# The value products of a pair of attention steps, issued at the end of the same pair instead of a pair later

## The chip, the cores and the metric

The kernel runs on one core of a Trainium2 chip. The metric is the device time of one execution in microseconds (us). Before the change three runs took 1965.31, 1966.28 and 1966.82 us; their median, 1966.28 us, is the time before. Five engines work side by side, each through its own list of instructions, in order: TensorE (PE, matmuls and transposes), ScalarE (ACT), VectorE (DVE), GpSimd (POOL) and SyncE (SP, which here issues nearly all DMAs). They wait for each other by semaphores.

## The reference, cut to what matters

Two layers of a decoder, each with forgetting attention and a gated MLP beside it. The change lies in the attention over the 1024 prompt positions:

```python
def fox_prompt(q, k, v, logf):                 # q, k, v: (1, 1024, 8 heads, 64)
    c = jnp.cumsum(logf, axis=1).transpose(0, 2, 1)
    def block(i):                              # 128 queries
        s = jnp.einsum('bqhd,bkhd->bhqk', qb, k) * HEAD_DIM ** -0.5
        s = s + (cb[..., :, None] - c[..., None, :])
        s = jnp.where(qpos[:, None] >= kpos[None, :], s, -jnp.inf)
        p = jax.nn.softmax(s, axis=-1)
        return jnp.einsum('bhqk,bkhd->bqhd', p, v)
```

The same stage also computes the input projections of q, k, v of the later pairs of heads, and the two gates `sigmoid(g_a)` and `sigmoid(g_b)` (as tanh) of the merge, which are 2 x 1024 columns of the input projection. These are independent of the attention and fill TensorE between its steps.

## The kernel before, in words

Every product in float32 is made of three matmuls (`three`, L76 to L78): each operand is split in a high part that TensorE takes at full rate and a low remainder. ScalarE makes the high part (a copy), VectorE or GpSimd the low one (a subtraction).

`attention_plan` writes the order of the attention stage as a list of small tasks. Each engine walks that same list and does its own share of each task, so the list sets the order on every engine at once. The tasks:

- `S h i`: scores of head h, 128 queries i, against the keys up to them: one or two chunks of at most 512 columns (PE L1324, L1326, mask L1329). VectorE adds the decay and takes the maximum (L1221, L1228), ScalarE the exponential (L1035), VectorE the division by the sum (L1121, L1122). The chunks use two PSUM banks in turn, so a third chunk waits until VectorE has taken the first.
- `T h G j`: transposes of the probabilities, keys j against the 512 queries of half G (PE L1341, 1 to 4 transposes). ScalarE copies the high part out of PSUM (L1045, tile `pthi`), VectorE the low one (L1237, tile `ptlo`). Two PSUM banks, three slots in SBUF.
- `V h G j`: the value products of that step (PE L1354 with the high part, L1355 with the low part), summed over j in one PSUM bank. The copy L1045 of a step waits until the V three steps earlier is done, for its slot.
- `O h G`: after the last V of a half, ScalarE copies one half of the sum (L1054, tile `ao`), VectorE adds the other (L1244), SP stores it.
- `Z p t`: q, k, v projections of 128 rows for a pair of heads (24 matmuls L76 to L78 on `aw_whi`), then copies and norms on ScalarE, VectorE, GpSimd; `X p t`: transposes of the normed q and k (PE L1301) with their splits (ACT L1015, DVE L1176, L1178).
- `P b c half`: a half-chunk of the gates, 12 matmuls L76 to L78 on `fhi`, `flo`. Two halves fill one PSUM bank, and ScalarE empties it by a tanh, `E` (L989, tile `th`). Z and P share two banks in turn: the first half of a chunk, or a Z, waits until the user two before it has been emptied.
- `G`, `W`, `Y`: loads and splits of weights; `D`: store of a tanh tile.

There are 96 steps (8 heads, 4 + 8 per head), taken two at a time: 48 pairs. In this text pair n is the one with steps 2n and 2n+1, from pair 0 to pair 47, in each of the two layers. Before the change a pair is: the `X` that is due, the two `T`, the `E` of what is unread, the two `V` **of the pair before** (and its `O`), then the scores and projections that are due, mixed with half-chunks, and half-chunks until the share of filling work is used. `LAG = 2` is the distance in steps between T and V. On PE that is

    X  T T  V V (of the pair before)  S .. Z .. P P P

## Time and profile before

| | |
|---|---|
| median of three runs | 1966.28 us |
| the profiled execution | 1964.39 us, of which span of the trace 1962.7 us |
| PE busy | 1904.7 us (97%) |
| DVE, ACT, POOL busy | 962.8, 677.1, 519.7 us |
| granted TensorE clock, mean | 0.993 |

The profile is of one execution. In a row of the timeline the first number is the start in us from the span's start, the second the duration; brackets name what ended an idle time before it. The ends of matmuls are modelled, and they overlap: from start to start a matmul of 384 columns takes 0.17 us though its row says 0.34. So distances on PE are taken here from start to start. The attention loop of the first layer runs from 114 us to 516 us, that of the second from 1080 us to 1481 us.

### The profile page before, as it was taken

The page shows a single profiled execution, that of the slowest core. Times are in us where ns is not written, and L with a number is a line of the kernel's source. Part 1 is how long each engine was busy: PE and PEld are TensorE (multiplying, and loading weights), DVE is VectorE, ACT ScalarE, POOL GpSimd, SP SyncE. Part 2 cuts the span into 40 slices and gives each one's busy share as a digit, 9 for nine tenths or more (in the row PEclk, how much of TensorE's full clock was granted, in tenths as well). Part 3 has the DMA queues.
Part 4 walks back from the last instruction along what each step waited for, and adds up shares of the span by engine and source line. Part 5 has one row for each costly group of instructions (what it writes and reads, how often), then busy time and mean ns, then how long its engine had stood idle before and what let it go on. Part 6 is the DMA issues. An engine that isn't in the chain of part 4 may idle for free.

```text
span 1962.7 us, 30986 instructions
## 1 busy us (share of the span) xinstructions
PE 1904.7 (97%) x11188; PEld 1755.5 (89%) x11188; DVE 962.8 (49%) x2296; ACT 677.1 (34%) x1487; POOL 519.7 (26%) x525
## 2 busy tenths in 40 slices
PE   5999999999999999999999999999999999999998
PEld 4999999999888889998789999999997888999986
DVE  5555665653264335455444565666433633455531
ACT  5344444444233222113224444454433332221120
POOL 3623333332021113111135233333311211231110
PEclk9999999999999999999999999999999999999999
DMA  5231313133215323525214213131322352226141
GB/s 155 58 108 52 94 54 96 47 88 84 64 39 158 91 62 87 196 84 167 97 55 111 59 48 99 44 106 49 106 58 62 79 147 77 76 83 232 39 172 54
DMA packets 217803, 178.39 MB, mean 91 GB/s; under 512 B 50260, under 2 KB 191076, under 8 KB 217652
## 3 DMA queue, kind: packets, MB, share of 16 engines
q1 hardware_dynamic: 217652, 176.41, 30.8%
q8 instruction: 90, 1.47, 0.3%
q14 instruction: 61, 0.50, 0.1%
HBM read 131.65 MB, written 44.71 MB: 90 GB/s over the span
## 4 chain that ended last, share of the span: by engine, by line
PE 85%; DMA 4%; DVE 3%; issue 2%; ACT 2%; SPq 1%; POOL 1%; POOLq 0%; DVEq 0%; ACTq 0%
PE bank L76 23%; PE bank L77 22%; PE bank L78 22%; PE bank L1341 3%; PE bank L1355 2%; PE bank L1301 2%; PE bank L1354 2%; PE bank L1324 2%; PE bank L1326 2%; PE bank L2108 2%; PE bank L2131 1%; DMA me_stage<-in_w_proj_b 1%; PE bank L2096 1%; DMA wo_stage<-in_w_out 1%; DVE at_prob L1221 1%
## 5 line engine op out<-in xcount | busy, mean ns | idle before, releaser
L76 PE MATMUL bank<-keep_hhi,at_fhi 128*128 128x384 f32 (+1 forms) x768 | 257.0, 335 | 3.4 <-ACT at_th L989 3.1
L78 PE MATMUL bank<-keep_hhi,at_flo 128*128 128x384 f32 (+1 forms) x768 | 251.3, 327 | 0.0
L77 PE MATMUL bank<-keep_hlo,at_fhi 128*128 128x384 f32 (+1 forms) x768 | 251.3, 327 | 0.0
L76 PE MATMUL bank<-aw_whi,keep_hhi 128*128 128x384 f32 (+3 forms) x576 | 198.5, 345 | 3.2 <-ACT at_th L989 1.3
L76 PE MATMUL bank<-keep_hhi,bw_whi 128*128 128x384 f32 (+1 forms) x576 | 196.3, 341 | 0.5 <-DVE br_th L1996 0.5
L77 PE MATMUL bank<-aw_wlo,keep_hhi 128*128 128x384 f32 (+3 forms) x576 | 195.5, 339 | 0.0
L78 PE MATMUL bank<-aw_whi,keep_hlo 128*128 128x384 f32 (+3 forms) x576 | 195.4, 339 | 0.0
L77 PE MATMUL bank<-keep_hlo,bw_whi 128*128 128x384 f32 (+1 forms) x576 | 189.4, 329 | 0.0
L78 PE MATMUL bank<-keep_hhi,bw_wlo 128*128 128x384 f32 (+1 forms) x576 | 189.2, 328 | 0.0
L1035 ACT ACTIVATE at_prob<-at_prob,at_nmx 128x128 f32<-128x128 f32 (+7 forms) x128 | 99.5, 778 | 239.0 <-DVE at_nmx L1228 238.9
L76 PEld LDWEIGHTS bank<-keep_hhi,at_fhi 128*128 128x128 f32 x768 | 144.4, 188 | 6.6 <-ACT at_th L989 5.3
L1237 DVE TENSOR_TENSOR at_ptlo<-bank,at_pthi 128x512 fp32r<-128x512 f32 x192 | 99.5, 550 | 98.6 <-ACT at_pthi L1045 97.3
L77 PEld LDWEIGHTS bank<-keep_hlo,at_fhi 128*128 128x128 f32 x768 | 144.7, 188 | 0.2
L78 PEld LDWEIGHTS bank<-keep_hhi,at_flo 128*128 128x128 f32 x768 | 144.3, 188 | 0.0
L1081 POOL TENSOR_TENSOR at_flo<-at_stage,at_fhi 128x512 fp32r<-128x512 f32 x64 | 85.8, 1340 | 170.2 <-ACT at_fhi L971 169.8
L1045 ACT ACTIVATE at_pthi<-bank 128x512 fp32r<-128x512 f32 x192 | 90.8, 491 | 73.7 <-PE bank L1341 62.4
L76 PE MATMUL bank<-ow_w,keep_hhi 128*128 128x512 f32 (+1 forms) x288 | 113.9, 395 | 0.7 <-issue 0.7
L78 PE MATMUL bank<-ow_w,keep_hlo 128*128 128x512 f32 (+1 forms) x288 | 114.2, 397 | 0.0
L77 PE MATMUL bank<-ow_w,keep_hhi 128*128 128x512 f32 (+1 forms) x288 | 113.8, 395 | 0.0
L76 PEld LDWEIGHTS bank<-keep_hhi,bw_whi 128*128 128x128 f32 x576 | 109.3, 190 | 4.0 <-issue 1.0
L76 PEld LDWEIGHTS bank<-aw_whi,keep_hhi 128*128 128x128 f32 (+1 forms) x576 | 105.5, 183 | 7.0 <-ACT at_th L989 1.8
L77 PEld LDWEIGHTS bank<-keep_hlo,bw_whi 128*128 128x128 f32 x576 | 109.3, 190 | 0.0
(252 smaller groups left out, 4300.7 us busy)
## 6 DMA issues: line engine op xcount, KB each, us to landing
at_stage<-in_w_in SPq DMA_DIRECT2D x160, 128.0 KB, 2.3
mg_gate<-gates SPq DMA_DIRECT2D x32, 544.0 KB, 5.2
gates<-at_th SPq DMA_DIRECT2D x64, 192.0 KB, 2.3
br_stage<-in_w_in SPq DMA_DIRECT2D x40, 256.0 KB, 3.2
at_stage<-in_w_in SPq DMA_DIRECT2D x48, 192.0 KB, 2.6
at_decay<-ncum SPq DMA_DIRECT2D x16, 512.0 KB, 3.8
br_k<-in_cache_k SPq DMA_DIRECT2D x32, 256.0 KB, 3.0
br_v<-in_cache_v SPq DMA_DIRECT2D x32, 256.0 KB, 3.0
```

What stands on the lines that cost most here:

```text
L76: nc.tensor.matmul(out, sh, mh, start=start and i == 0, stop=False)
L77: nc.tensor.matmul(out, sh, ml, start=False, stop=False)
L78: last = nc.tensor.matmul(out, sl, mh, start=False, stop=stop and i == n - 1)
L1035: nc.scalar.activation(prob[:, blk(i):blk(i) + w], prob[:, blk(i):blk(i) + w], ACT.Exp, bias=nmx[:, si % 2:si % 2 + 1], accum_out=sm[:, si ...
L1045: nc.scalar.activation(pt_hi[:, ti % (LAG + 1), lo:512], tps[ti % 2][:, lo:512], ACT.Copy).then_inc(t_hi, 1)
L1081: nc.gpsimd.tensor_tensor(flo[:, fu % NF, :], stage[:, slot[s], :], fhi[:, fu % NF, :].bitcast(F32), ALU.subtract).then_inc(w_lo_p, 1)
L1237: nc.vector.tensor_tensor(pt_lo[:, ti % (LAG + 1), lo:512], tps[ti % 2][:, lo:512], pt_hi[:, ti % (LAG + 1), lo:512].bitcast(F32), ALU.sub ...
L1301: last = nc.tensor.transpose(xps[:, at:at + n], qn[0:n, 2 * i + hh, :, :].rearrange("p e d -> p (e d)"), g.ident[0:n, 0:n])
L1324: nc.tensor.matmul(sps[cc % 2][:, 0:w], qk[:, h % NHEAD, 0, q], qk[:, h % NHEAD, 1, ks], start=True, stop=False)
L1326: last = nc.tensor.matmul(sps[cc % 2][:, 0:w], qk[:, h % NHEAD, 0, q], k_lo[:, h % NHEAD, ks], start=False, stop=not diagonal)
L1341: last = nc.tensor.transpose(tps[ti % 2][:, r * P:(r + 1) * P], prob[:, at:at + P], g.ident[:, :])
L1354: nc.tensor.matmul(ops[:, lo:512], pair, pt_hi[:, ti % (LAG + 1), lo:512], start=j == 0, stop=False)
```

## The change

The loop over the pairs ends one pass earlier, and the `V` of a pair (with its `O`) is put behind that pair's own scores, projections and half-chunks. Only these lines of `attention_plan` differ; the number of instructions stays the same on every engine.

```diff
-    for n in range(0, len(steps) + LAG, 2):
+    for n in range(0, len(steps), 2):
         due = after.pop(n, []) + after.pop(n + 1, [])
...
         plan += [("T",) + s for s in steps[n:n + 2]]
         fill.read(0)
-        for h, G, j in steps[max(0, n - LAG):n - LAG + 2]:
-            plan.append(("V", h, G, j))
-            if j == 4 * G + 3:
-                plan.append(("O", h, G))
         while scores or projections:
...
         while spent + fill.at - first < total * (n + 2) / (len(steps) + 1) and fill.at < len(fill.pieces):
             fill.half()
+        for h, G, j in steps[n:n + 2]:
+            plan.append(("V", h, G, j))
+            if j == 4 * G + 3:
+                plan.append(("O", h, G))
```

A pair on PE is now `X  T T  S .. Z .. P P P  V V (of this pair)`. Since the V of a pair and the T of the next one have nothing between them but an X, the order of PE as a whole changes only in this: at each start of a pair, the X and the two T change places with the two V.

TensorE at the start of pair 12 (head 2, first half, keys 0 and 1), `-` before and `+` after. L77 and L78 are the end of the filling work of pair 11, L1341 the T of pair 12, L1354 and L1355 the V of pair 11, L1324 the scores of pair 12:

```order
 L77 MATMUL bank<-keep_hlo,at_fhi 128x320
 L78 MATMUL bank<-keep_hhi,at_flo 128x320
-L1341 MATMUL bank<-keep_ident,at_prob 128x128 x7
 L1354 MATMUL bank<-at_pthi,at_vsplit 128x256
 L1355 MATMUL bank<-at_ptlo,at_vsplit 128x256
 L1354 MATMUL bank<-at_pthi,at_vsplit 128x128
 L1355 MATMUL bank<-at_ptlo,at_vsplit 128x128
+L1341 MATMUL bank<-keep_ident,at_prob 128x128 x7
 L1324 MATMUL bank<-at_qk 128x512
 L1326 MATMUL bank<-at_klo,at_qk 128x512
```

The seven transposes move behind the four value matmuls, right in front of the scores; the scores and everything up to the next start of a pair stay where they were.

ScalarE at the same place. L1045 are the copies of the two T of pair 12, L989 the tanh of the two chunks that pair 11 left unread, L1054 the output copy of head 1; before the change:

```order
L1045 ACTIVATE at_pthi<-bank 128x512
L1045 ACTIVATE at_pthi<-bank 128x384
L989 ACTIVATE at_th<-bank 128x384 x2
L1054 ACTIVATE at_ao<-bank 64x512
```

The same stretch of ScalarE's list after the change:

```order
L1054 ACTIVATE at_ao<-bank 64x512
L1045 ACTIVATE at_pthi<-bank 128x512
L1045 ACTIVATE at_pthi<-bank 128x384
L989 ACTIVATE at_th<-bank 128x384 x2
```

The output copy moves ahead of the two copies of P and the tanh; nothing else moves on ScalarE here. On VectorE the sum L1244 likewise moves ahead of the X and T of the next pair:

```order
-L1176 TENSOR_TENSOR at_qk<-bank,at_qk 64x2x128
-L1178 TENSOR_TENSOR at_klo<-bank,at_qk 128x2x128
-L1237 TENSOR_TENSOR at_ptlo<-bank,at_pthi 128x512
-L1237 TENSOR_TENSOR at_ptlo<-bank,at_pthi 128x384
-L1244 TENSOR_TENSOR at_ao<-bank,at_ao 64x512
+L1244 TENSOR_TENSOR at_ao<-bank,at_ao 64x512
+L1176 TENSOR_TENSOR at_qk<-bank,at_qk 64x2x128
+L1178 TENSOR_TENSOR at_klo<-bank,at_qk 128x2x128
+L1237 TENSOR_TENSOR at_ptlo<-bank,at_pthi 128x512
+L1237 TENSOR_TENSOR at_ptlo<-bank,at_pthi 128x384
```

Here one instruction moves past four; the scores behind them keep their place. SP's stores of `ao` move in the same way; GpSimd's list does not change.

Of the kernel before, what the change touches and what calls it, by code (L numbers as in the profile page):

```python
# [562 lines left out]
LAG = 2  # L563
# [65 lines left out]
def attention_plan():  # L629

    plan = []
    fill = Filler(plan)
    for t in range(NT):
        plan.append(("Z", 0, t))
        if t >= 2:  # L640
            plan.append(("X", 0, t - 2))
        if t >= 3:
            fill.weights(min(t - 2, NF))
    plan += [("F",)]
    fill.half()
    plan += [("X", 0, NT - 2)]
    fill.half()
    fill.half()
    fill.read(0)
    plan += [("W", 1, k) for k in range(2)]  # L650
    fill.half()
    plan += [("X", 0, NT - 1), ("C",), ("N", 0)]
    for i in range(1, 4):
        fill.half()
        fill.read(0)
        plan += [("W", 1, k) for k in (2 * i, 2 * i + 1)]
        fill.half()
    fill.read(0)
    plan += [("S", 0, 0), ("S", 0, 1)]
    fill.half()  # L660
    plan += [("S", 0, 2)]
    fill.half()
    fill.read(0)
    plan += [("S", 0, 3)]
    fill.half()
    fill.half()
    after = {}
    PER = 12

    def put(n, *steps):  # L670
        after.setdefault(n, []).extend(steps)

    for h in range(H):
        for i, off in enumerate((-10, -9, -8, -6, -4, -3, -2, 0)):
            if h or i >= 4:
                put(max(0, PER * h + off), ("S", h, i))
    for p in range(1, PAIRS):
        at = [3, 5, 7, 9, 11, 13, 15, 17, 19]
        for t, n in zip(range(NT - len(at), NT), at):
            n += 2 * PER * (p - 1)  # L680
            put(n, ("Z", p, t))
            if t and ("X", p, t - 1) not in plan:
                put(n, ("X", p, t - 1))
        put(n + 2, ("X", p, NT - 1))
        if p + 1 < PAIRS:
            for k in range(KT):
                put(n + 1 + 2 * (k // 3), ("W", p + 1, k))
        else:
            for u in range(KT):
                put(n + 2 + 2 * u, ("Y", u))  # L690
    steps = [(h, G, j) for h in range(H) for G in range(2) for j in range(4 * G + 4)]
    first = fill.at
    total = sum(2 * (s[0] == "Z") for v in after.values() for s in v) + len(fill.pieces) - first
    spent = 0
    turned = []
    for n in range(0, len(steps) + LAG, 2):
        due = after.pop(n, []) + after.pop(n + 1, [])
        plan += turned
        turned = [s for s in due if s[0] == "X"]
        scores = [s for s in due if s[0] == "S"]  # L700
        projections = [s for s in due if s[0] == "Z"]
        plan += [("T",) + s for s in steps[n:n + 2]]
        fill.read(0)
        for h, G, j in steps[max(0, n - LAG):n - LAG + 2]:
            plan.append(("V", h, G, j))
            if j == 4 * G + 3:
                plan.append(("O", h, G))
        while scores or projections:
            if scores:
                s = scores.pop(0)  # L710
                plan.append(s)
                if s[2] == PT_ - 1 and s[1] + 1 < H:
                    plan.append(("N", s[1] + 1))
            if projections:
                fill.before_z()
                spent += 2
                plan.append(projections.pop(0))
            elif scores:
                fill.half()
        plan += [s for s in due if s[0] in "WY"]  # L720
        while spent + fill.at - first < total * (n + 2) / (len(steps) + 1) and fill.at < len(fill.pieces):
            fill.half()
    fill.end()
    assert not after
    return plan


def attention_phase(nc, l, g):
    plan = attention_plan()
    R = Region(nc, "at", g.free_attention)  # L730
    S = g.sem("a", l)
# [1742 lines left out]
```

How the kernel before makes its waits and increments, by code:

```python
def all_through(eng, g):  # L119
    eng.wait_ge(g.pe_through, g.phases)
    eng.wait_ge(g.act_through, g.phases)
    eng.wait_ge(g.dve_through, g.phases)
    eng.wait_ge(g.pool_through, g.phases)
    eng.wait_ge(g.sp_through, g.phases)
# [54 lines left out]
    @block.sync  # L181
    def _(sp):
        sp.dma_start(g.gains[0:DEPTH, :], norm_g[:, :]).then_inc(gains_in, 16)
        sp.dma_start(g.gains[DEPTH:DEPTH + 1, :], norm_g[0:1, :]).then_inc(gains_in, 16)
        for t in range(NT):
            if t >= NX:
                sp.wait_ge(hn_r, t - NX + 1)
                sp.wait_ge(ss_r, t - NX + 1)
            sp.dma_start(xt[0:ROWS[t], t % NX, :], x_rows(g, t)).then_inc(x_in[t % NX], 16)
            if t == 0:
                sp.wait_ge(gains_in, 32)
                sp.dma_start(gain[:, :], g.gains[0:1, :].to_broadcast([P, D])).then_inc(consts, 16)
            if t >= 3:
                load_pair(sp, g, 0, 0, t - 3, stage[:, t - 3, :], w_in[t - 3])
        for k in range(NT - 3, KT):
            load_pair(sp, g, 0, 0, k, stage[:, k, :], w_in[k])
        sp.sem_inc(g.sp_through, 1)
# [3 lines left out]
        def square(t):  # L201
            if t >= NT:
                return
            act.wait_ge(x_in[t % NX], 16 * (t // NX + 1))
            if t:
                act.wait_ge(ss_r, t)
            if t >= NR:
                act.wait_ge(ms_r, t - NR + 1)
            nc.scalar.activation(sqj[0:ROWS[t], :], xt[0:ROWS[t], t % NX, :], ACT.Square,
# [84 lines left out]
    @block.tensor  # L294
    def _(pe):
        pe.wait_ge(made, 3)
        for t in range(NT):
```

## Rows read from the trace of the kernel before

**Rows 1.** Waits of PE, whole span: who, for whom; us, times, longest.
```profile
PE bank L76 <- ACT at_th L989: 4.4, 8, 1.0
...
PE bank L1324 <- DVE at_mx L1221: 3.7, 6, 1.0
```

**Rows 2.** ScalarE's copy L1045: what ended the idle time before it, us, times.
```profile
  PE bank L1355: 8.9, 34
```

**Rows 3.** Timeline of PE, start of pair 12: transposes, then the gate half-chunk.
```profile
220.11 0.93 PE L1341 MATMUL bank<-keep_ident,at_prob 128*128 128x128 f32 x7
...
222.33 0.41 PE L76 MATMUL bank<-keep_hhi,at_fhi 128*128 128x384 f32 x1
```

**Rows 4.** Timeline of ScalarE, start of pair 12: copies of P, tanh.
```profile
220.75 1.12 ACT L1045 ACTIVATE at_pthi<-bank 128x512 fp32r<-128x512 f32 x2 [0.50 <-PE bank L1341]
221.76 0.82 ACT L989 ACTIVATE at_th<-bank 128x384 f32<-128x384 f32 x2
```

**Rows 5.** Timeline of PE, end of pair 47: last value products, last half-chunk.
```profile
513.40 0.28 PE L1354 MATMUL bank<-at_pthi,at_vsplit 128*128 128x256 f32 x1
...
513.81 0.36 PE L76 MATMUL bank<-keep_hhi,at_fhi 128*128 128x320 f32 x1
```

**Rows 6.** Timeline of ScalarE, same place: the output copy behind them.
```profile
514.01 0.59 ACT L1054 ACTIVATE at_ao<-bank 64x512 f32<-64x512 f32 x1 [1.68 <-PE bank L1355]
```

**Rows 7.** Timeline of PE, start of pair 37: T, V, S, P.
```profile
428.96 0.49 PE L1341 MATMUL bank<-keep_ident,at_prob 128*128 128x128 f32 x3
429.20 0.48 PE L1354 MATMUL bank<-at_pthi,at_vsplit 128*128 128x512 f32 x1
...
430.11 0.22 PE L1324 MATMUL bank<-at_qk 128*128 128x128 f32 x1
...
430.73 0.41 PE L76 MATMUL bank<-keep_hhi,at_fhi 128*128 128x320 f32 x1 [0.17 <-ACT at_th L989]
```

**Rows 8.** Timeline of ScalarE, start of pair 37.
```profile
429.37 0.38 ACT L1045 ACTIVATE at_pthi<-bank 128x256 fp32r<-128x256 f32 x1 [1.47 <-PE bank L1341]
430.02 0.28 ACT L1045 ACTIVATE at_pthi<-bank 128x128 fp32r<-128x128 f32 x1 [0.26 <-PE bank L1355]
430.19 0.87 ACT L989 ACTIVATE at_th<-bank 128x384 f32<-128x384 f32 x2
```

**Rows 9.** Timeline of PE, start of pair 39.
```profile
444.83 1.03 PE L1341 MATMUL bank<-keep_ident,at_prob 128*128 128x128 f32 x8
...
447.45 0.41 PE L76 MATMUL bank<-keep_hhi,at_fhi 128*128 128x320 f32 x1
```

**Rows 10.** Timeline of PE, start of pair 44.
```profile
483.62 1.04 PE L1341 MATMUL bank<-keep_ident,at_prob 128*128 128x128 f32 x8
...
486.02 0.45 PE L76 MATMUL bank<-keep_hhi,at_fhi 128*128 128x384 f32 x1 [0.96 <-ACT at_th L989]
```

**Rows 11.** Timeline of PE, start of pair 47.
```profile
505.66 0.49 PE L1341 MATMUL bank<-keep_ident,at_prob 128*128 128x128 f32 x3
...
507.37 0.44 PE L76 MATMUL bank<-keep_hhi,at_fhi 128*128 128x384 f32 x1 [0.41 <-ACT at_th L989]
```

**Rows 12.** Timeline of ScalarE, start of pair 39: the tanh.
```profile
446.92 0.87 ACT L989 ACTIVATE at_th<-bank 128x384 f32<-128x384 f32 x2
```

**Rows 13.** Timeline of VectorE, pair 26: its two low parts of P.
```profile
340.78 1.27 DVE L1237 TENSOR_TENSOR at_ptlo<-bank,at_pthi 128x512 fp32r<-128x512 f32 x2
```

**Rows 14.** Timeline of PE: the start of pair 27.
```profile
344.04 0.60 PE L1301 MATMUL bank<-keep_ident,at_qn 128*128 128x128 f32 x4
```

**Rows 15.** Timeline of VectorE, pair 34: first chunk of the first scores.
```profile
408.21 0.68 DVE L1221 CUSTOM_DVE_ANT_0 at_prob<-bank,at_decay 128x512 f32<-128x512 f32 x1
```

**Rows 16.** Timeline of PE, pair 34: its second scores.
```profile
409.32 0.39 PE L1324 MATMUL bank<-at_qk 128*128 128x512 f32 x1
```

**Rows 17.** Busy time by stretch: us, PE PEld DVE ACT POOL (x), PEclk, DMA, GB/s.
```profile
480.00:500.00 20.00, 19.04 (x123) 18.50 (x122) 4.14 (x6) 6.40 (x13) 2.56 (x2) 1.00 0.18 53
...
1504.00:1510.00 6.00, 6.00 (x27) 5.36 (x28) 3.55 (x11) 1.35 (x3) 0.54 (x1) 0.78 0.01 3
```

## The prediction

> **What bounds the kernel now.** First the busy times in the small table: PE is busy 97% of the span, no other engine more than half of it. So time can be won or lost almost only where PE stands still or does other work. The change adds no work to PE, so I looked at PE's waits next: over both layers the attention loop has only two kinds. A gate half-chunk waits for a tanh that empties its bank, 4.4 us in 8 places, and scores wait for VectorE, 3.7 us in 6 places [rows 1]. Both layers show the same places at the same distance from the loop's start, so I work out one layer and double it. Last I read the timelines of PE, ScalarE and VectorE over all 48 pairs of a layer.
>
> **What the change moves.** The lists show that nothing is moved between the scores and the end of the filling work of a pair. PE keeps its whole cycle and only exchanges, at each start of a pair, the X and T with the value products of the pair before. Seen from the scores and half-chunks, X and T are issued later by the length of these value products, v; seen from X and T, the scores and half-chunks arrive v earlier. What hung on the value products loses nothing: they leave in front of T instead of behind it, and the bank of their sum is free long before the next half begins.
>
> The length v. The pair with keys 256 and 128 columns wide is at 513.40 to 513.81, so v = 0.41 us [rows 5]. In pair 37 the V of 512 and 384 columns take 429.20 to 430.11, 0.91 us, but that includes some 0.08 us that the first matmul behind transposes takes longer than its width; the scores will now pay that in its place. So v = 0.83 us, and by columns (1792 in 0.83 us) 0.95 us for two steps of 512 (2048) [rows 7].
>
> **What is waited for behind T.** ScalarE's queue behind T is copy, copy, tanh (and a second tanh where two chunks are unread). This chain is the same in both kernels; only the cover that PE has in front of the half-chunk shrinks by v. One thing gets better: before, the second copy needs its slot in SBUF back from a V that stood behind T on PE, 8.9 us in 34 places [rows 2]. Now this V stands ahead of T and the copy starts as soon as ScalarE is free.
>
> I write t for the start of T, p for the start of the first half-chunk or Z that needs a tanh issued in this pair, and R for the time from T to the release of the bank. A tanh start is followed by PE after 0.54 us in pair 37 (430.19 to 430.73) [rows 7, 8], and I use 0.54 where it is 384 wide. The new start is t + v + R, if that is later than the undisturbed p. The added time is v + R - (p - t). I went through the 48 pairs: only where two chunks are unread at the start, and the first user of a bank comes right behind T or one score, is the cover this short. That is seven pairs of a layer; elsewhere either a second half (1.75 us or more) or a whole Z stands in between.
>
> - **Pairs 12, 24 and 42** (one score of two chunks ahead of the half-chunk). T at 220.11, half-chunk at 222.33: p - t = 2.22 us [rows 3]. Copy at 220.75, tanh at 221.76, which is T + 1.65, plus 0.54: R = 2.19 us [rows 4]. Today this fits with 0.03 us to spare, and PE does not stall at all. These pairs now also have the output copy L1054 ahead of the copies of P. It starts 0.61 us behind the first value matmul (513.40 to 514.01) [rows 5, 6], which is T + 0.20, and takes 0.59 us in its row, some 0.53 until the next can start. So the first copy begins at T + 0.73 in place of T + 0.64, and R becomes 2.28. Added: 0.41 + 2.28 - 2.22 = 0.47 us each, 1.41 us together.
> - **Pair 37**: p - t = 1.77 us [rows 7]. First copy at T + 0.41; the second waited until T + 1.06 for V and now follows the first after some 0.32 us; tanh 0.17 us after it as today: T + 0.90, R = 1.44 [rows 8]. Added: 0.83 + 1.44 - 1.77 = 0.50 us.
> - **Pair 39**: p - t = 2.62 us [rows 9]. The tanh starts at T + 2.09, because the second copy waits for V; without that wait the copies follow each other as in pair 12, the second at T + 1.19, and the tanh comes 0.50 us behind: R = 2.23 [rows 4, 12]. Added: 0.95 + 2.23 - 2.62 = 0.56 us.
> - **Pair 44**, with an output copy: p - t = 2.40 us [rows 10]. Its second copy is not held up much, R stays at about 2.39. Added: 0.41 + 2.39 - 2.40 = 0.40 us.
> - **Pair 47**: p - t = 1.71 us [rows 11]. R as in pair 37, with a narrower tanh, 1.39. Added: 0.83 + 1.39 - 1.71 = 0.51 us.
>
> Sum of a layer: 1.41 + 0.50 + 0.56 + 0.40 + 0.51 = 3.4 us; both layers 6.8 us.
>
> **What I cost at nothing.** The scores that wait for VectorE: a second score of two chunks behind one half-chunk. In pair 34 VectorE has taken the first chunk at 408.89, PE comes at 409.32 [rows 15, 16]. X is 0.95 us later, but in the timeline VectorE is then still busy with the tail of a Z, so by my estimate only 0.15 us of this reach the scores, and 0.28 us remain. Pairs 10 and 40 have no more at stake, and pair 22 hangs on the same tail. The bounds: 0 if VectorE's tail covers it, 0.7 us each (0.95 less the margin) if not, 6 places, 4 us. I take 0, since the rows show the tail.
>
> The new wait of V for its own low part: V now comes at the end of its pair. The tightest is pair 26: the low parts end at 342.05, the next pair starts at 344.04 [rows 13, 14], and V will be there 0.5 us earlier (v of the short V that goes ahead), 1.5 us behind the low part. Behind V would be queued all of PE. Lower bound 0, upper bound some 1 us in two places if VectorE ran a whole operation more late. I take 0.
>
> The output sum L1244 in front of X and T on VectorE costs its 0.7 us to the low parts of 7 pairs per layer; they have the rest of the pair as cover. SP waits for that sum at the end of a pair, where stores of q and k wait anyway, and the weight loads behind it come a pair ahead of their use. The last tanhs come after the last half-chunk as before; the one of the second last bank comes behind the output copy, while PE runs its last 1.75 us of half-chunk. The exchange itself (which matmul stands behind the transposes) may be worth some hundredths per pair, up to 1 us either way over 96 pairs.
>
> Against its own time the profiled execution goes from 1964.39 to 1971.2 us. It is 1.9 us below the median; the median goes from 1966.28 to 1973.1 us.
>
> **The clock.** The new stalls are of the kind that the row of 480 to 500 us already holds: with one of 0.96 us in it, the granted clock reads 1.00 there, 2.4 GHz [rows 10, 17]. After a longer stall of the next stage, ahead of 1504 us, the row reads 0.78, that is 0.44 of 6 us at 1.2 GHz and 1.3 us lost [rows 17]. The Trainium skill (TensorE: Matmul & The Clock Gate, on thin matmuls, where queues are cycled through PSUM) says that frequent short idling between groups of matmuls can make the gate swing between its levels and cost throughput. By that rule this change would be worse than I say; the row of 480 to 500 us does not agree with it for a stall of this size.
>
> **The rivals.**
> - *The released slot wins more than the cover loses: faster.* The place is ScalarE's second copy behind T. If the chain behind T shortened by more than v, the tanh stalls would go. It decides from R below p - t - v: below 1.81 us in pair 12, 0.94 us in pair 37. All 8 stalls gone would give 1966.3 - 4.4 = 1961.9 us. For it: the 34 waits. Against it: in pair 37 the wait is 0.33 us of the copy, v is 0.83 us. Chance 0.07.
> - *Nothing to be seen.* ScalarE catches up, or gains elsewhere offset this; 1966 us, within 0.2%. For it: PE's stalls are few and the work is the same. Chance 0.11.
> - *Only the pairs that stall today get longer.* Pairs 12, 24 and 42 keep their fit, 37, 39, 44 and 47 lose 1.97 us a layer: 1970.2 us, on the edge of 0.2%. Against it: the margin of 0.03 us. Chance 0.10.
> - *VectorE's margins are used up as well*: scores in pairs 10, 34, 40 or V in pair 26 wait; up to 4 us more, 1977 us. Chance 0.08.
> - *The clock falls at the 14 places*: 14 x 1.3 = 18 us more, 1991 us. Against it the row at 480 us. Chance 0.02.
>
> **How the numbers follow.** The forecast, 1973.1 us, has 0.62. A difference of 0.2%, 3.9 us, is about what a measurement can tell from none. The range goes from 1968.0 (the third rival with half its size) to 1978.5 (the fourth and the small unknown of the exchange). Slower by more than 0.2%: 0.62 less a little for a forecast that comes out at half, half of the third rival, and the last two, 0.74. Within: 0.19. Faster: 0.07.
>
> **What would show it.** In the changed kernel's timeline the half-chunks of pairs 12, 24 and 42 have a wait for the tanh L989 of about 0.5 us that they do not have now; the total of that wait grows from 4.4 us to some 11 us, with 14 or more places, and the longest becomes 1.4 us (pair 44). ScalarE's wait for L1355 ahead of L1045 is gone. V never waits for L1237. The loop of a layer is 3.4 us longer. I am wrong if the tanh waits do not grow, or if they grow and the span does not, or if PE has new waits at L1354 or more at L1324.

## The result and the profile after

| | before | after |
|---|---|---|
| median | 1965.8 us (6 runs, 1961.8 to 1967.02) | 1973.55 us (6 runs, 1971.71 to 1979.76) |
| profiled execution: time, span | 1964.39, 1962.7 us | 1972.24, 1970.5 us |
| loop of the first layer | 401.66 us | 405.59 us |
| loop of the second layer | 401.73 us | 405.68 us |

The change makes the kernel slower: ratio 1.0046, 95% interval 1.0033 to 1.0058. The forecast was 1973.1 us, in a range of 1968.0 to 1978.5 us. "Loop" is here the time on PE from the first transposes of pair 0 to the first matmul of the next stage (`sw_w`), from start to start. The two loops grew by 7.9 us together and the span by 7.8 us; the rest of the program came out even, within 0.1 us.

Busy time and waits of PE after (page, section 1; waits of PE over the whole span). They answer to the small table of before and to [rows 1]:

```profile
PE 1905.0 (97%) x11188; PEld 1754.3 (89%) x11188; DVE 957.1 (49%) x2296; ACT 673.2 (34%) x1487; POOL 519.1 (26%) x525
```

```profile
PE bank L76 <- ACT at_th L989: 11.8, 17, 1.3
...
PE bank L1324 <- DVE at_mx L1221: 3.8, 7, 1.0
```

PE does the same work (1905.0 against 1904.7 us), it only stands still longer, and nearly all of it for the tanh: 11.8 us in 17 places against 4.4 us in 8. The wait for VectorE at the scores stayed, but for one new wait of 0.20 us in pair 0 of the second layer; in a second execution of the same kernel (`after_again`, below) it is not there. One of the 17 lies ahead of the second loop (0.77 us), where the change moves nothing, so the loops hold 11.1 us. Pair 1 waits 0.65 us in each layer, before and after. What ended the idle time ahead of ScalarE's copies of P, after:

```profile
  PE bank L1341: 70.9, 18
```

The line for L1355 of [rows 2] has gone: the copies never wait for their slot now. So the change did free what it could free, and lost more. In pair 24 the second copy of P now starts 0.50 us behind the first; before it was 0.63 us, and by the modelled ends of PE the V that frees its slot ended 0.10 us ahead of it.

Pair 24 after, PE (transposes T, score chunks, half-chunk) and ScalarE:

```profile
323.48 0.95 PE L1341 MATMUL bank<-keep_ident,at_prob 128*128 128x128 f32 x7
324.18 0.48 PE L1324 MATMUL bank<-at_qk 128*128 128x512 f32 x1
...
325.70 0.42 PE L76 MATMUL bank<-keep_hhi,at_fhi 128*128 128x320 f32 x1 [0.28 <-ACT at_th L989]
```

```profile
323.68 0.59 ACT L1054 ACTIVATE at_ao<-bank 64x512 f32<-64x512 f32 x1 [0.29 <-PE bank L1355]
324.29 0.98 ACT L1045 ACTIVATE at_pthi<-bank 128x512 fp32r<-128x512 f32 x2
325.15 0.88 ACT L989 ACTIVATE at_th<-bank 128x384 f32<-128x384 f32 x2
```

This is the shape of [rows 3, 4] after the change. T is again the start of the transposes. The output copy starts at T + 0.20, as forecast, the first copy of P at T + 0.81 (0.73 was forecast: the output copy holds ScalarE for 0.61 us, not 0.53), the tanh at T + 1.67 (1.74 was forecast: the released slot lets the second copy follow sooner), and PE goes on at T + 2.22. PE stands 0.28 us, in a place where it did not stand before.

The seven places of the first layer (us). The waits are those printed beside the half-chunk; the printed wait leaves out some 0.15 us of what PE loses from start to start. The added time is the length of the pair on PE, from its first instruction to the first one of the next pair, after less before. The second layer repeats the waits within 0.01 us, but for pair 12 with 0.87 us; its added time there is 1.04 us, and that of the six others is the same within 0.02 us.

| pair | wait before | wait after | added, pair to pair | forecast |
|---|---|---|---|---|
| 12 | none | 1.04 | 1.32 | 0.47 |
| 24 | none | 0.28 | 0.45 | 0.47 |
| 42 | none | 0.29 | 0.43 | 0.47 |
| 37 | 0.17 | 0.63 | 0.46 | 0.50 |
| 39 | none printed (0.31 lost from start to start) | 0.59 | 0.45 | 0.56 |
| 44 | 0.96 | 1.28 | 0.34 | 0.40 |
| 47 | 0.41 | 0.86 | 0.55 | 0.51 |
| sum | | | 4.00 | 3.38 |

Five places came out 0.02 to 0.11 us under the forecast, pair 47 0.04 us over it, and pair 12 by 0.85 us (0.57 us in the second layer). Of the 3.93 us by which this loop grew, the rest is 0.15 us over the other pairs and 0.23 us less in pair 0, which changed by 0.05 us the other way in the second layer. Pair 12 after, ScalarE:

```profile
219.26 0.53 ACT L964 ACTIVATE aw_whi<-at_stage 128x392 fp32r<-128x392 f32 x1 [0.26 <-DMA at_stage<-in_w_in]
220.15 0.53 ACT L964 ACTIVATE aw_whi<-at_stage 128x392 fp32r<-128x392 f32 x1 [0.36 <-DMA at_stage<-in_w_in]
220.59 0.61 ACT L971 ACTIVATE at_fhi<-at_stage 128x512 fp32r<-128x512 f32 x1
221.23 0.59 ACT L1054 ACTIVATE at_ao<-bank 64x512 f32<-64x512 f32 x1
221.84 0.98 ACT L1045 ACTIVATE at_pthi<-bank 128x512 fp32r<-128x512 f32 x2
```

Here ScalarE is behind: it waits for two weight loads and splits what they brought and one more unit, so the output copy starts 0.96 us after the transposes (220.27), not 0.20.

### The profile page after: what moved, and what is told of

It reads as the page before. It is cut to its first block, busy times and chain, and to the rows that moved or that the text cites. A ratio compares the mean times of both kernels' runs of the same rounds, so it can differ in the third digit from the quotient of the medians.

```text
span 1970.5 us, 30986 instructions
## 1 busy us (share of the span) xinstructions
PE 1905.0 (97%) x11188; PEld 1754.3 (89%) x11188; DVE 957.1 (49%) x2296; ACT 673.2 (34%) x1487; POOL 519.1 (26%) x525
## 4 chain that ended last, share of the span: by engine, by line
PE 83%; DMA 4%; DVE 4%; issue 3%; ACT 2%; SPq 1%; POOL 1%; POOLq 0%; DVEq 0%; ACTq 0%
PE bank L76 23%; PE bank L77 22%; PE bank L78 22%; PE bank L1341 3%; PE bank L1355 2%; PE bank L1354 2%; PE bank L1301 2%; PE bank L2108 2%; PE bank L2131 1%; PE bank L1326 1%; PE bank L1324 1%; DMA me_stage<-in_w_proj_b 1%; PE bank L2096 1%; DVE at_prob L1221 1%; DMA wo_stage<-in_w_out 1%
## 5 line engine op out<-in xcount | busy, mean ns | idle before, releaser
L77 PE MATMUL bank<-keep_hlo,at_fhi 128*128 128x384 f32 (+1 forms) x768 | 251.9, 328 | 0.0
L78 PE MATMUL bank<-keep_hhi,at_flo 128*128 128x384 f32 (+1 forms) x768 | 251.9, 328 | 0.0
L77 PE MATMUL bank<-aw_wlo,keep_hhi 128*128 128x384 f32 (+3 forms) x576 | 195.8, 340 | 0.0
L78 PE MATMUL bank<-aw_whi,keep_hlo 128*128 128x384 f32 (+3 forms) x576 | 195.6, 340 | 0.0
L77 PE MATMUL bank<-keep_hlo,bw_whi 128*128 128x384 f32 (+1 forms) x576 | 189.3, 329 | 0.0
L78 PE MATMUL bank<-keep_hhi,bw_wlo 128*128 128x384 f32 (+1 forms) x576 | 189.1, 328 | 0.0
L77 PEld LDWEIGHTS bank<-keep_hlo,at_fhi 128*128 128x128 f32 x768 | 145.1, 189 | 0.0
L78 PEld LDWEIGHTS bank<-keep_hhi,at_flo 128*128 128x128 f32 x768 | 144.6, 188 | 0.0
L78 PE MATMUL bank<-ow_w,keep_hlo 128*128 128x512 f32 (+1 forms) x288 | 114.4, 397 | 0.0
L77 PE MATMUL bank<-ow_w,keep_hhi 128*128 128x512 f32 (+1 forms) x288 | 114.0, 396 | 0.0
L77 PEld LDWEIGHTS bank<-keep_hlo,bw_whi 128*128 128x128 f32 x576 | 109.3, 190 | 0.0
L78 PEld LDWEIGHTS bank<-keep_hhi,bw_wlo 128*128 128x128 f32 x576 | 109.0, 189 | 0.0
```

The lines of the kernel that those rows point to most:

```text
L77: nc.tensor.matmul(out, sh, ml, start=False, stop=False)
L78: last = nc.tensor.matmul(out, sl, mh, start=False, stop=stop and i == n - 1)
```

## The experiments

Line numbers in the rows of some experiments are shifted by 3 or 6 against the kernel before, since their planners have more lines. The loop lengths and waits are from the profiled execution of each. The waits are of the whole span: in every run but `before` one of them, of 0.55 to 0.85 us, lies ahead of the second loop.

| kernel | loop, layer 1 | loop, layer 2 | PE waits for tanh | ratio to before |
|---|---|---|---|---|
| before | 401.66 | 401.73 | 4.4 us, 8 | |
| after | 405.59 | 405.68 | 11.8 us, 17 | 1.0046 (1.0033 to 1.0058) |
| seven | 404.76 | 405.57 | 11.3 us, 17 | 1.0037 (1.0025 to 1.0048) |
| others | 402.23 | 402.43 | 5.4 us, 11 | 1.0007 (0.9997 to 1.0017) |
| after_tanh_first | 400.12 | 399.79 | 1.8 us, 6 | 0.9982 (0.9972 to 0.9991) |
| before_tanh_first | 398.96 | 398.95 | 1.1 us, 3 | 0.9974 (0.9963 to 0.9985) |
| not_10_11 | 405.03 | 405.55 | 11.1 us, 17 | single run |
| after_sum_late | 404.69 | 404.60 | 8.8 us, 13 | single run |
| after_again | 405.55 | 405.60 | 12.0 us, 17 | single run |
| seven_again | 404.76 | 404.94 | 10.5 us, 17 | single run |

**seven and others: the change cut in two.** The theory says that seven places of a layer carry the cost, its rival that the exchange costs a little everywhere. In the kernel before, the value products are put in front of X and T where `early` holds. The diff shows both lines that set `early`; each kernel has one of them:

```diff
+        values = []
+        for h, G, j in steps[max(0, n - LAG):n - LAG + 2]:
+            values.append(("V", h, G, j))
+            if j == 4 * G + 3:
+                values.append(("O", h, G))
+        early = n // 2 in (12, 24, 37, 39, 42, 44, 47)      # seven
+        early = n < 96 and n // 2 not in (12, 24, 37, 39, 42, 44, 47)   # others
+        if early:
+            plan += values
         plan += turned
...
-        for h, G, j in steps[max(0, n - LAG):n - LAG + 2]:
...
+        if not early:
+            plan += values
```

> The kernel before, with the value products of the preceding pair in front of X and T at pairs 12, 24, 37, 39, 42, 44 and 47 alone; the other pairs keep the old order. Theory (the cover in front of a tanh is what costs): nearly all of the loss comes back, each layer some 3.2 us longer than before, 6 to 7 us in all (ratio 1.003 to 1.0035), the wait of PE for the tanh L989 grows from 4.4 us to 10 to 11 us. Pair 12 should wait only 0.5 us, not the 1.04 us of the changed kernel, if its excess comes from the T of pairs 10 and 11 being late. Rival (the exchange itself costs about the same at each of the 47 places, 0.08 us each): 14 of 94 places, 1.2 us, ratio 1.0006, and the waits stay near 4.4 us.

> The complement: the value products stand in front of X and T at all pairs except 12, 24, 37, 39, 42, 44, 47 (and the last). Theory: the cover in front of the seven tanhs is as before, waits for L989 4 to 5 us, time within 1.5 us of before (ratio 0.9995 to 1.0007); if the late weight splits reach pair 12 as well, its half-chunk waits up to 0.5 us per layer. Rival (even cost of the exchange): 80 of 94 places, 6.7 us, ratio 1.0034.

Measured: with seven places alone the kernel takes 1973.08 us in the median (8 runs), with all the others 1967.26 us (12 runs), against 1965.6 us of before (29 runs). PE waits for the tanh 11.3 us in the first and 5.4 us in the second, where 10 to 11 us and 4 to 5 us had been expected.

By the loops, the seven places make 3.1 and 3.8 us of a layer, the 40 others 0.6 and 0.7 us; the sum is that of the full change (3.9) within 0.6 us. Of the 3.8 us some 0.8 us are a late weight load at pair 24, which is taken up below; `seven_again` has 3.1 and 3.2 us. The even cost is refuted: it wanted 1.2 us from the seven and 6.7 us from the others. What the others cost is not spread either. Pair 12 is 0.42 and 0.46 us longer in this kernel, with a new wait of 0.21 and 0.26 us, although V stands behind T there; pair 24 of the second layer is 0.20 us longer. The 40 pairs that changed their order cost some 0.15 us a layer together, and that is what the exchange itself costs.

**after_tanh_first and before_tanh_first: the tanh ahead of the copies of P.** If the cover in front of the tanh is what is missing, the tanh need not stand behind T at all: its chunks have long been full. The same edit was made in both kernels, and changes ScalarE's list alone:

```diff
-        plan += [("T",) + s for s in steps[n:n + 2]]
         fill.read(0)
+        plan += [("T",) + s for s in steps[n:n + 2]]
```

> The changed kernel with the tanhs of the unread chunks ahead of the two copies of P on ScalarE; only ScalarE's order differs. Theory: the wait for the tanh falls from 11.8 us to about 1 us (what is left in pair 1, behind the exponential of 1024 columns), so the time goes from 7.8 us over the kernel before to some 3 us under it, ratio 0.9985. Rival (the copies of P now come 0.5 to 0.9 us later, and PE waits for VectorE at the scores L1324 or at V instead): the wait at L1324 grows from 3.8 us by 2 us or more or one appears at L1354, and the time ends at 1.000 to 1.003.

> The kernel before with the tanhs of the unread chunks ahead of the two copies of P on ScalarE; only ScalarE's order differs. Theory: its 4.4 us of waits for the tanh fall to about 1 us, 3.4 us less, ratio 0.9983; then the place of the value products is worth nothing and this kernel and the changed one with the same edit differ by less than 1 us. Rival (late copies of P cost at the scores): no gain or a loss of 1 to 2 us.

Measured: 1961.32 us (12 runs) and 1960.39 us (10 runs), both clear of the time before (1965.6 us) by their intervals, though small. That is 4.3 and 5.2 us less, where some 3 and 3.4 us had been expected. The waits, after_tanh_first and then before_tanh_first, whose wait at L1324 is the same 4.5 us:

```profile
PE bank L1324 <- DVE at_mx L1221: 4.5, 8, 1.0
...
PE bank L76 <- ACT at_th L989: 1.8, 6, 0.6
```

```profile
PE bank L76 <- ACT at_th L989: 1.1, 3, 0.7
```

The rival is there but small: late copies of P add 0.8 us of waits at the scores (3.7 to 4.5 us). The loop of the changed kernel shrinks by 5.5 and 5.9 us, that of the kernel before by 2.7 and 2.8 us. In the kernel before the gain is where PE stood for the tanh: 0.45 us in pair 1, 0.37 in 37, 0.37 in 39, 1.18 in 44 and 0.59 in 47, less 0.35 us that pair 0 waits longer for VectorE. It is more than the printed waits, on which the expectation went, because these leave out some 0.15 us each and the one of pair 39 altogether. So the order of two kinds of task on ScalarE decided what the place of V costs. It does not become nothing: 1.2 and 0.9 us of a layer are left between the two loops, where I expected less than 1 us in all. Pair 44 holds 0.64 and 0.53 us of it, pair 12 0.44 and 0.19 us. ScalarE in pair 44, first after_tanh_first, then before_tanh_first:

```profile
483.83 0.59 ACT L1054 ACTIVATE at_ao<-bank 64x512 f32<-64x512 f32 x1 [1.48 <-PE bank L1355]
484.45 0.82 ACT L989 ACTIVATE at_th<-bank 128x384 f32<-128x384 f32 x2
```

```profile
482.02 0.48 ACT L989 ACTIVATE at_th<-bank 128x384 f32<-128x384 f32 x1
483.19 0.44 ACT L989 ACTIVATE at_th<-bank 128x320 f32<-128x320 f32 x1 [0.69 <-PE bank L78]
```

With V at the end of the pair, the output copy is written ahead of the tanh and waits 1.48 us for the last V, and the tanh, whose chunk is full, stands behind it. In the other kernel the first tanh runs during the half-chunks, 2.2 us earlier against the end of these. PE waits 0.30 us for it in the first and not at all in the second.

**after_sum_late: the output copy.** In the changed kernel `O` is held back and put behind the next pair's T and tanhs. This moves VectorE's sum and SP's store along with ScalarE's copy:

```diff
         plan += [("T",) + s for s in steps[n:n + 2]]
         fill.read(0)
+        plan += sums
+        sums = []
...
             if j == 4 * G + 3:
-                plan.append(("O", h, G))
+                sums.append(("O", h, G))
+    plan += sums
     fill.end()
```

> The changed kernel with each output sum O (ScalarE L1054, VectorE L1244, SP's store) back behind the T and tanhs of the next pair; V stays at the end of its pair. Theory: the output copy ahead of the copies of P is worth 0.1 us where ScalarE was idle (pairs 24, 42, 44: waits 0.28, 0.29, 1.28 fall by 0.1 to 0.2 us) and its full 0.5 us in pair 12, where ScalarE is behind; the total for L989 falls from 11.8 to about 10 us and the span by 1.5 to 2 us. Rival (all of the loss is the output copy's): the waits of pairs 24 and 42 vanish and the total falls below 6 us.

Measured, in a single run: 1971.2 us, the loops 0.9 and 1.1 us shorter than the changed kernel's (together 2.0 us, of the span 1.0 us; 1.5 to 2 us had been expected), the tanh waits 3.0 us less (8.8 us, where about 10 had been expected). The wait of pair 12 fell from 1.04 and 0.87 us to 0.16 and none, that of pair 44 from 1.28 to 1.12, those of pair 42 and, in the first layer, pair 24 went below what is printed. So the output sum in front is worth about 1 us of the 3.9 us of a layer, more than the forecast's 0.09 us in each of three pairs; pair 12 alone became 0.99 and 0.75 us shorter. It is ScalarE's copy that does this, and no earlier load: with the sum held back the last two weight splits ahead of the chain of pair 12 start within 0.13 us of where they start in the changed kernel. The rest is the cover. The total did not fall below 6 us, and the rival is refuted.

**not_10_11, after_again, seven_again: the excess of pair 12.** I supposed that pairs 10 and 11, where ScalarE splits eight units of weights between its copies of P, pass the lateness of their T on to pair 12. `not_10_11` has `early = n < 96 and n // 2 not in (10, 11)`; the other two are second executions of the changed kernel and of `seven`, to see what repeats.

> The changed order at all pairs but 10 and 11, where the value products stay behind T (and the last pair, as before). Theory (the excess in pair 12 comes from the late T of pairs 10 and 11, by way of ScalarE's weight splits and the three slots of the staging ring): the wait of pair 12's half-chunk for the tanh falls from 1.04 and 0.87 us to about 0.3 us in both layers, all other waits as in the changed kernel, total for L989 some 10.6 us. Rival (the excess comes from the late arrival of a weight load of this one execution): it stays at 0.9 to 1.0 us in at least one layer.

> The changed kernel once more, for a second profiled execution. Theory (late T of pairs 10 and 11 delay ScalarE's weight splits): the half-chunk of pair 12 waits 0.8 to 1.1 us in both layers again. Rival (the weight loads land at a different time in each execution, and ScalarE is behind only where one is late): the waits of pairs 12 and 24 scatter between 0.28 and 1.1 us from execution to execution and from layer to layer; the other five places repeat to 0.02 us.

> The kernel with the new order at the seven pairs alone once more, for a second profiled execution. Theory: pair 12 waits 0.29 us in both layers again. Rival: pair 12 or pair 24 shows another wait than the first time (0.29, 0.29 and 0.28, 1.11 us), by 0.2 us or more.

| waits for the tanh, first and second layer | pair 12 | pair 24 |
|---|---|---|
| after | 1.04, 0.87 | 0.28, 0.28 |
| after_again | 0.94, 0.88 | 0.28, 0.44 |
| seven | 0.29, 0.29 | 0.28, 1.11 |
| seven_again | 0.29, 0.29 | 0.28, 0.46 |
| not_10_11 | 0.29, 0.29 | 0.28, 0.87 |

With pairs 10, 11 and 12 in the new order pair 12 waits 0.87 to 1.04 us in all four layers of the table, and with pairs 10 and 11 in the old one 0.29 us in all six. That bears out the theory for pair 12, and the traces show the way. ScalarE's exponential of pair 11, before and after:

```profile
216.77 1.04 ACT L1035 ACTIVATE at_prob<-at_prob,at_nmx 128x896 f32<-128x896 f32 x1 [1.59 <-DVE at_nmx L1228]
```

```profile
217.44 1.04 ACT L1035 ACTIVATE at_prob<-at_prob,at_nmx 128x896 f32<-128x896 f32 x1 [1.59 <-DVE at_nmx L1228]
```

It waits for VectorE's maximum, which stands behind the low parts of T in VectorE's list. Pair 12 starts on PE at 220.11 before and 219.87 after, so the exponential starts 3.34 us ahead of it before and 2.43 us after: 0.91 us later, about the length of the value products that went ahead of T. Pair 10 has the same: its first exponential starts 3.98 us behind T in both kernels, so it moved with T. The weight splits stand behind the exponential. The first split behind it starts 2.30 us ahead of pair 12 before, as in `seven` and `not_10_11` (2.29 to 2.31), and 1.38 or 1.39 us ahead in the changed kernel, `others` and `after_sum_late`. The last load that ScalarE waits for there is issued 3.41 us ahead of pair 12 before and 2.48 us after. By the code a load needs a slot that a split has freed, and the splits of pairs 10 and 11 come as much later too.

Pair 24 in the second layer has an excess too, of a size that changes with the execution and with no relation to the order of the pairs ahead of it. In `not_10_11` ScalarE shows what it is:

```profile
1293.24 0.63 ACT L977 ACTIVATE at_fhi<-at_stage 128x512 fp32r<-128x512 f32 x1 [1.09 <-DMA at_stage<-in_w_in]
1293.89 0.59 ACT L1060 ACTIVATE at_ao<-bank 64x512 f32<-64x512 f32 x1
1294.51 0.98 ACT L1051 ACTIVATE at_pthi<-bank 128x512 fp32r<-128x512 f32 x2
```

A weight load lands late, its split stands ahead of the output copy and the copies of P, and all of it is in the tanh's chain. In this kernel the split starts 0.13 us after T, and in the three other layers with an excess from 0.30 us ahead of T to 0.37 us after it; in those with 0.28 us of wait it starts 0.45 to 1.04 us ahead. In the kernel before it is late in the second layer as well, 0.15 us after T against 0.42 us ahead of it, but costs nothing there. The rival is right for pair 24; why the load lands late there stays open. The other five places repeat within 0.01 us in all these executions. The time of after_again was 1970.11 us, of seven_again 1971.65 us and of not_10_11 1973.27 us; single times scatter by as much as these kernels differ.

## Why the prediction was right, and where it was not

*The exchange on PE and the chain on ScalarE.* Right. The changed profile has the new waits at pairs 12, 24 and 42, longer ones at 37, 39, 44 and 47, the longest at pair 44 (1.28 us, 1.4 was forecast), and, but for the 0.20 us at scores in pair 0 of one execution, at no other place of the loop. `seven` and `others` show that these places carry it. The measure v + R - (p - t) gave each of six places within 0.11 us.

*The sum.* 6.8 us were forecast, the medians differ by 7.75 us and the loops by 7.9 us. The mis-sized term is pair 12: 0.47 us for it, 1.32 and 1.04 us measured. The step that failed was the release time R, taken with ScalarE idle ahead of the chain: 2.28 us forecast, 2.99 and 2.81 us measured. The statement that weight loads come a pair ahead of their use was wrong there, ScalarE waited for them (in [rows 4] it is idle for only 0.50 us ahead of the copies), and what the later T of pairs 10 and 11 does to VectorE and ScalarE was not followed on to pair 12. The output copy was mis-sized with it: 0.61 us of ScalarE instead of 0.53, and all of it in the chain when ScalarE is behind. Against this the other six places together came out 0.23 us lower in a layer: 2.91 us forecast, 2.68 us measured. R was 0.03 to 0.08 us shorter there than forecast; in pairs 24 and 42 the second copy followed 0.13 us sooner once its slot was free, which had been counted in pairs 37, 39 and 47 alone. The exchange itself was worth 0.15 us of a layer, for which a bound of 1 us in all had been left. That 1973.55 us lies only 0.45 us from the forecast is in part luck: the change cost 0.95 us more than said, and the median before, of six runs, lies 0.5 us under that of three.

*What was cost at nothing.* The scores of pair 34 met VectorE in time: the first chunk was taken at 410.61 and PE came at 410.91, without a wait. V never waited for its low part. In pair 26 (VectorE, then PE, after):

```profile
342.68 1.27 DVE L1237 TENSOR_TENSOR at_ptlo<-bank,at_pthi 128x512 fp32r<-128x512 f32 x2
```

```profile
345.53 0.39 PE L1354 MATMUL bank<-at_pthi,at_vsplit 128*128 128x512 f32 x1
```

The low parts ended at 343.95, 1.6 us ahead of V; 1.5 had been forecast. But that VectorE's lateness behind a later T costs nothing holds for its own waits only: it came back through ScalarE in pair 12.

*The rivals.* That the released slot wins was refuted: the waits for it went and the tanh waits grew. "Nothing to be seen" and "only the pairs that stall today" are refuted by the three new places. VectorE's margins held at the places named. More waits at L1324 were a sign of being wrong; the changed kernel has one of 0.20 us, at pair 0, in one of its two traces. The clock did not fall: the mean of the granted clock is 0.994 after against 0.993 before, and both loops read 1.00, 2.4 GHz. The first:

```profile
114.00:520.00 406.00, 398.31 (x2468) 381.75 (x2467) 215.28 (x637) 174.84 (x407) 130.37 (x122) 1.00 0.25 69
```

The Trainium skill (TensorE: Matmul & The Clock Gate, A second HAM failure mode: psum-queue depth-cycling) tells of a kernel in which TensorE idled shortly between groups of matmuls so often that its clock went back and forth between its levels, at a cost in throughput; its matmuls had 512 columns and were not thin, as the prediction has it. The trace here shows no such swing, with 16 stalls of 0.28 to 1.28 us for the tanh spread over some 800 us; no run here has more frequent ones.

## What to carry to other kernels

When work is moved from behind an instruction to in front of it on a full engine, little is gained or lost by the work itself (0.15 us a layer here); look for what the passed instruction starts, and whether anything behind it is waited for before that chain is through. The cost of a place is v + R - (p - t): the length of what went ahead, plus the chain's time to release, less the distance there was; and R has to be taken with the helper engine as busy as it is there, loads and all, and as late as the move itself has made it in the steps ahead. Where a chain has a member that depends on nothing in it (here a tanh of a chunk long full, behind two copies of fresh transposes), put that member first: that alone took the kernel before from 1965.6 to 1960.4 us, ratio 0.9974 (0.9963 to 0.9985). It also took most of the cost out of the move: with the tanh first the medians of the two orders are 0.9 us apart, without it 7.75 us.

## What the runs showed that I had not expected

A late weight load reaches TensorE through a queue that has nothing to do with the weights waited for: in four of the ten layers of the table above, all of them second layers, PE stood 0.44 to 1.11 us at pair 24 against 0.28 us, since the split of a late load held up ScalarE with the copies of P and a ready tanh behind it. Five of the seven places repeat to 0.01 us over executions and kernels, while whole times scatter by 5 us (1957.94 to 1963.13 us for before_tanh_first). Between `after` and `after_again`, two executions of one kernel, the two loops together differ by 0.12 us and the times by 2.13 us. So most of that scatter lies outside this loop; what it is stays open.
